# Merged prologues for the projections of a two-block model, with the layer-norm rows on GpSimd behind the last low part

## The reference, cut to what matters

```python
y = gelu(ssm(u) + d_skip * u)
z = y * sigmoid(y @ w_glu + b_glu)
return z @ w_out                      # end of the S5 mixer
z = silu(layernorm(conv(z), ln_g, ln_b))
return z @ w_out + b_out              # end of the convolution mixer
```

## Time and the profile before

| what | us |
|---|---|
| median of the runs | 3826.11 |
| lowest and highest of three | 3824.54, 3830.32 |
| the profiled execution | 3831.06 |
| its span in the trace | 3829.3 |

### The profile page before, as it was taken

One profiled execution on the slowest core, in us unless ns is written; L12 is line 12 of the kernel. 1 busy time (PEld: TensorE's weight loads), 2 busy tenths in 40 slices (PEclk: granted clock), 3 DMA queues, 4 the chain that ended last, 5 costly groups with the idle time before them and its releaser, 6 DMA issues. The chain is left out here.

```text
span 3829.3 us, 64659 instructions
## 1 busy us (share of the span) xinstructions
PE 3380.1 (88%) x20742; PEld 2962.7 (77%) x20742; DVE 2483.6 (65%) x4673; ACT 1672.9 (44%) x3310; POOL 1252.5 (33%) x1096
## 2 busy tenths in 40 slices
PE   8988699999459998798899999987888889999997
PEld 7963489898349986598678999976668877899996
DVE  7979578786958644569954555554355986455555
ACT  4430344445034453344744444444344465444443
POOL 2426112120612100038863333320002976433333
PEclk9985699999579998899999999988688999999999
DMA  5520278685028642344055555544113413555554
GB/s 181 192 89 0 80 258 322 236 326 185 6 100 304 232 163 96 121 140 151 11 170 170 183 186 185 185 150 140 39 55 127 154 44 132 169 185 185 185 186 148
DMA packets 163122, 590.78 MB, mean 154 GB/s; under 512 B 18596, under 2 KB 19364, under 8 KB 162728
## 3 DMA queue, kind: packets, MB, share of 16 engines
q1 hardware_dynamic: 143824, 521.92, 40.1%
q10 hardware_dynamic: 19160, 67.18, 4.7%
HBM read 587.96 MB, written 1.06 MB: 154 GB/s over the span
## 5 line engine op out<-in xcount | busy, mean ns | idle before, releaser
L314 PE MATMUL ps<-hT,parts 128*128 128x256 f32 x12864 | 1630.1, 287 | 108.4 <-DVE parts L138 53.4
L314 PEld LDWEIGHTS ps<-hT,parts 128*128 128x128 f32 x12864 | 1610.7, 195 | 146.5 <-DVE parts L138 58.4
L138 DVE TENSOR_TENSOR parts<-ring,parts 128x512 fp32r<-128x512 f32 x1786 | 1187.4, 700 | 603.3 <-ACT parts L133 594.3
L133 ACT ACTIVATE parts<-ring 128x512 fp32r<-128x512 f32 x1930 | 1156.8, 628 | 624.8 <-PE ps L314 584.8
L314 PE MATMUL ps<-parts,gatedT 128*128 128x512 f32 x4128 | 1008.7, 397 | 8.0 <-DVE parts L138 7.9
L314 PEld LDWEIGHTS ps<-parts,gatedT 128*128 128x128 f32 x4128 | 760.2, 189 | 174.8 <-POOL gatedT L982 8.3
L1118 POOL TENSOR_TENSOR gatedT<-acted,iota 128x256 fp32r<-128x256 f32 x264 | 197.2, 747 | 1434.3 <-PE ps L314 1166.7
L1089 ACT ACTIVATE acted<-ps 128x256 f32<-128x256 f32 x264 | 102.1, 387 | 594.6 <-PE ps L314 594.6
L1121 POOL TENSOR_TENSOR gatedT<-acted,gatedT 128x256 fp32r<-128x256 f32 x264 | 311.1, 1178 | 20.7
L1102 DVE TENSOR_TENSOR acted<-acted,big 128x256 f32<-128x256 f32 x176 | 74.9, 426 | 361.2 <-ACT acted L1089 361.2
L314 PE MATMUL ps<-parts,hT 128*128 128x512 f32 (+2 forms) x1056 | 245.4, 396 | 66.4 <-DVE parts L138 66.4
(11 more groups left out here) (294 smaller groups left out, 2420.0 us busy)
## 6 DMA issues: line engine op xcount, KB each, us to landing
ring<-wts SPq DMA_DIRECT2D x965, 512.0 KB, 3.4
big<-mod_wts ACTq DMA_DIRECT2D x112, 512.0 KB, 5.0
big<-rows SPq DMA_DIRECT2D x15, 512.0 KB, 5.3
big<-mod_bias ACTq DMA_DIRECT2D x14, 512.0 KB, 5.6
big<-mod_rows SPq DMA_DIRECT2D x4, 512.0 KB, 4.6
big<-peer_keys SPq DMA_DIRECT2D x2, 1024.0 KB, 5.1
x<-x_in SPq DMA_DIRECT2D x1, 1024.0 KB, 5.2
big<-s_bc ACTq DMA_DIRECT2D x4, 256.0 KB, 3.2
```

Source lines behind the costliest of these rows:

```text
L133: act.activation(self.part(n, half, 0), self.raw(n, half), ACT.Copy).then_inc(self.hi_done, 1)
L138: v.tensor_tensor(self.part(n, half, 1), self.raw(n, half), self.part(n, half, 0).bitcast(F32), ALU.subtract).then_inc(self.lo_done, 1)
L314: last = pe.matmul(out, a(x), b(y), start=start and x + y == 0, stop=stop and x == 1)
```

## The change

It has these parts:

1. `turn(n)` is false for n under 5, so the additions and all loads but the first two of each feed-forward come later.
2. `ModEntry`: even pieces get their value from ACT, odd pieces from DVE (a new step, `e_odd`), and the turned pieces lie in other banks, so that the two engines read different ones. `e_turned` counts four pieces instead of two.
3. The layer-norm rows on POOL wait for the eighth low part (`e_lo`), not for the transposes.
4. 22 warm matmuls instead of 18, 24 where there is a layer norm.
5. `SplitEntry` can make sum and gelu piece by piece, splits the first weight tile at its start if nothing did, and the second one after the fifth piece. `project_rows` takes an entry.
6. S5: sum, gelu and split become the entry of the sigmoid projection; the gating product is made per piece beside it (`finish`); it splits one tile ahead; the rows projection gets a `SplitEntry`. The rows projections of convolution and NSA get one too.
7. The stage before NSA's query projection splits the first tile of that projection ahead.

```diff
@@ -60,7 +60,7 @@
...
 HELD = 40
-WARM = 18
+WARM, WARM_LN = 22, 24
 GATES = (2, 5, 10, 13)
@@ -398,7 +398,7 @@
...
     def __init__(self, k, pre, post=False, coef=1.0, bias=False):
-        self.k, self.pre, self.post, self.coef, self.bias = k, pre, post, coef, bias
+        self.k, self.pre, self.post, self.coef, self.bias, self.more = k, pre, post, coef, bias, None
@@ -507,13 +507,16 @@
...
-    sems = "e_gained e_squared e_rooted e_updated e_inverse e_normed e_turned e_value e_hi e_lo e_dve e_rows"
+    sems = "e_gained e_squared e_rooted e_updated e_inverse e_normed e_turned e_value e_odd e_hi e_lo e_dve e_rows"
...
     def turned(self, kc):
-        return self.k.ps[:, kc // 2, (kc % 2) * T:(kc % 2) * T + T]
+        at = kc // 2 % 2 * T
+        return self.k.ps[:, kc // 4 + kc % 2 * 2, at:at + T]
@@ -546,14 +549,24 @@
...
                 k.w.split_hi(act, first + n)
-            for kc in range(KC + 1):
-                if kc < KC:
-                    act.wait_ge(s["e_turned"], kc // 2 + 1)
-                    act.activation(self.value(kc), self.turned(kc), ACT.Identity, scale=k.gain[:, self.norm, 0, kc:kc + 1],
-                                   bias=k.gain[:, self.norm, 1, kc:kc + 1]).then_inc(s["e_value"], 1)
-                if kc:
-                    act.wait_ge(s["e_value"], kc)
-                    act.activation(k.hT[:, 0, kc - 1, :], self.value(kc - 1), ACT.Copy).then_inc(s["e_hi"], 1)
+            def even(kc):
+                act.wait_ge(s["e_turned"], kc // 4 + 1)
+                act.activation(self.value(kc), self.turned(kc), ACT.Identity, scale=k.gain[:, self.norm, 0, kc:kc + 1],
+                               bias=k.gain[:, self.norm, 1, kc:kc + 1]).then_inc(s["e_value"], 1)
+            def high(kc):
+                if kc % 2:
+                    act.wait_ge(s["e_odd"], kc // 2 + 1)
+                else:
+                    act.wait_ge(s["e_value"], kc // 2 + 1)
+                act.activation(k.hT[:, 0, kc, :], self.value(kc), ACT.Copy).then_inc(s["e_hi"], 1)
+            even(0)
+            even(2)
+            for kc in range(0, KC, 2):
+                high(kc)
+                high(kc + 1)
+                if kc + 4 < KC:
+                    even(kc + 4)
@@ -598,12 +611,16 @@
...
             for kc in range(KC):
+                if kc % 2 == 0:
+                    v.wait_ge(s["e_turned"], kc // 4 + 1)
+                    v.tensor_scalar(self.value(kc + 1), self.turned(kc + 1), k.gain[:, self.norm, 0, kc + 1:kc + 2],
+                                    k.gain[:, self.norm, 1, kc + 1:kc + 2], ALU.mult, ALU.add).then_inc(s["e_odd"], 1)
                 v.wait_ge(s["e_hi"], kc + 1)
...
         def _(pe):
-            warm(k, pe, first, WARM)
+            warm(k, pe, first, WARM_LN if ln else WARM)
             for tt in range(TT):
@@ -614,13 +631,13 @@
...
                     last = pe.transpose(self.turned(kc)[:, tt * P:(tt + 1) * P], k.x[:, tt, kc * P:(kc + 1) * P], k.ident[:, :])
-                    if tt == TT - 1 and kc % 2 == 1:
+                    if tt == TT - 1 and kc % 4 == 3:
                         last.then_inc(s["e_turned"], 1)
...
             if ln:
-                pool.wait_ge(s["e_turned"], 4)
+                pool.wait_ge(s["e_lo"], KC)
                 for n, op in ((1, ALU.mult), (2, ALU.add)):
@@ -638,24 +655,47 @@
...
-    sems = "e_hi e_lo"
-    def __init__(self, k, src):
-        self.k, self.src, self.more = k, src, None
+    sems = "e_sum e_func e_hi e_lo"
+    def __init__(self, k, src, other=None):
+        self.k, self.src, self.other, self.more = k, src, other, None
...
     def enter(self, s, block, first, done):
-        k, src = self.k, self.src
+        k, src, other = self.k, self.src, self.other
...
         def _(act):
-            for n in range(done, 2):
-                k.w.split_hi(act, first + n)
+            def gelu(kc):
+                act.wait_ge(s["e_sum"], kc + 1)
+                act.activation(src[:, kc, :], src[:, kc, :], ACT.Gelu_apprx_tanh).then_inc(s["e_func"], 1)
+            if done < 1:
+                k.w.split_hi(act, first)
+            if other is not None:
+                gelu(0)
             for kc in range(KC):
+                if other is not None:
+                    if kc + 1 < KC:
+                        gelu(kc + 1)
+                    act.wait_ge(s["e_func"], kc + 1)
                 act.activation(k.hT[:, 0, kc, :], src[:, kc, :], ACT.Copy).then_inc(s["e_hi"], 1)
+                if kc == KC // 2 and done < 2:
+                    k.w.split_hi(act, first + 1)
...
         def _(v):
+            def add(kc):
+                v.tensor_tensor(src[:, kc, :], src[:, kc, :], other[:, kc, :], ALU.add).then_inc(s["e_sum"], 1)
+            if other is not None:
+                add(0)
+                add(1)
+            if done < 1:
+                k.w.split_lo(v, first)
             for kc in range(KC):
+                if other is not None and kc + 2 < KC:
+                    add(kc + 2)
                 v.wait_ge(s["e_hi"], kc + 1)
@@ -668,10 +708,12 @@
...
-def splitting(k, block, first, n, after=None, act_first=None, entry=None, ahead=0):
+def splitting(k, block, first, n, after=None, act_first=None, entry=None, ahead=0, beside=None):
...
     done_hi = max(done, 2) if entry else done
+    if isinstance(entry, SplitEntry):
+        done = max(done, 1)
     k.w.split_to = first + n + ahead
@@ -696,9 +738,18 @@
...
                 k.w.split_lo(v, first + j, i)
-        rounds(v, n, RING, tile)
+        if beside:
+            for f in range(n):
+                if f >= done:
+                    k.w.split_lo(v, first + f)
+                beside(v, f)
+        else:
+            rounds(v, n, RING, tile)
         if ahead:
             k.w.split_lo(v, first + n)
+        if beside:
+            for f in range(n, n + 3):
+                beside(v, f)
@@ -729,7 +780,7 @@
...
-def project_columns(k, n, evacuate, early=(), entry=None):
+def project_columns(k, n, evacuate, early=(), entry=None, ahead=0, finish=None):
@@ -753,17 +804,26 @@
...
             evacuate(act, f, k.ps[:, 4 + f % 4, 0:T]).then_inc(s["stored"], 1)
-            if entry and isinstance(entry, ModEntry) and entry.more and f < KC:
+            if entry and entry.more and f < KC:
                 entry.more_columns(act, s, f)
-        splitting(k, block, first, n, after, entry=entry)
-def project_rows(k, groups=1, evacuate=None, start=True, stop=True, ahead=0, late=()):
+        def finished(v, f):
+            if f >= 3:
+                v.wait_ge(s["stored"], f - 2)
+                finish(v, f - 3)
+        beside = finished if finish else None
+        splitting(k, block, first, n, after, entry=entry, ahead=ahead, beside=beside)
+def project_rows(k, groups=1, evacuate=None, start=True, stop=True, ahead=0, late=(), entry=None):
...
     first = k.w.take(n)
-    with stage(k, "stored") as (s, block):
+    with stage(k, "stored " + (entry.sems if entry else "")) as (s, block):
+        if entry:
+            entry.enter(s, block, first, k.w.split_before(first))
         @block.sync
@@ -775,6 +835,8 @@
...
                     pe.wait_ge(s["stored"], 4 * (g - 1))
+                if entry:
+                    pe.wait_ge(s["e_lo"], f + 1)
                 row_product(k, pe, first + f, lambda tt, half: k.ps[:, 4 * (g % 2) + 2 * tt + half, :],
@@ -786,7 +848,7 @@
...
                         evacuate(act, g, tt, half, k.ps[:, 4 * (g % 2) + 2 * tt + half, :]).then_inc(s["stored"], 1)
-        splitting(k, block, first, n, after if evacuate else None, ahead=ahead)
+        splitting(k, block, first, n, after if evacuate else None, ahead=ahead, entry=entry)
@@ -828,7 +890,7 @@
...
     def turn(self, n):
-        return n % 3 != 1
+        return n >= 5 and n % 3 != 1
@@ -1438,25 +1500,12 @@
...
-    with stage(k, "sum") as (s, block):
-        @block.vector
-        def _(v):
-            v.tensor_tensor(yT, yT, cy, ALU.add).then_inc(s["sum"], 1)
-        @block.scalar
-        def _(act):
-            act.wait_ge(s["sum"], 1)
-            act.activation(yT, yT, ACT.Gelu_apprx_tanh)
-    split_columns(k, yT)
-    project_columns(k, KC, lambda act, f, ps: act.activation(uT[:, f, :], ps, ACT.Sigmoid, bias=col(k, "s5_b_glu", f)))
-    with stage(k, "gated") as (s, block):
-        @block.vector
-        def _(v):
-            v.tensor_tensor(yT, yT, uT, ALU.mult).then_inc(s["gated"], 1)
-    split_columns(k, yT)
-    project_rows(k, ahead=1, late=row_loads(k, "post01"))
+    def gate(v, f):
+        v.tensor_tensor(yT[:, f, :], yT[:, f, :], uT[:, f, :], ALU.mult)
+    project_columns(k, KC, lambda act, f, ps: act.activation(uT[:, f, :], ps, ACT.Sigmoid, bias=col(k, "s5_b_glu", f)),
+                    entry=SplitEntry(k, yT, cy), ahead=1, finish=gate)
+    project_rows(k, ahead=1, late=row_loads(k, "post01"), entry=SplitEntry(k, yT))
@@ -1536,8 +1585,7 @@
...
```

(11 more changed lines are left out.)

## The result

| | median us | lowest, highest | runs | span in the profile |
|---|---|---|---|---|
| before | 3828.22 | 3824.54, 3830.39 | 4 | 3829.3 |
| after | 3784.34 | 3781.10, 3786.17 | 4 | 3779.3 |

The ratio is 0.9885, with a 95% interval of 0.9868 to 0.9903: 43.9 us faster by the medians, where 45.2 was forecast. The interval is 6 to 7 us to either side. The two profiled executions differ by 50.0, since that of before was one of the slower ones of its kernel and that of after the fastest of its own. So I compare steps: the time from one landmark of PE (first warm matmul of a stage, first product) to the next, in both traces. The step of a feed-forward runs from its first warm matmul to that of the next stage, the step of a layer-norm entry from its first warm matmul to the first matmul behind its projection.

A forecast was written before the change was run, and what follows sets the result against it. PE, busy 88% of the span, was taken as the bound, with gains only from its idle or half-clock time. Terms 16.3 + 8.1 + 10.6 + 10.7 - 0.5 = 45.2 us, off the median 3826.11, gave 3781, range 3766 to 3800.

The forecast's parts named there:

- Part 1: Three feed-forward starts: with slots 0 to 4 empty, PE's gap before the second tile goes; 16.3 us gained.
- Part 2: Three layer-norm entries: rows moved behind the last low part hold up weight splits instead; 2.7 us each, 8.1 gained.
- The first rival: Layer-norm entries: the splits don't contend with the rows, three times 3.7 us more, 3770; 12%.
- Part 3: End of S5: 4.3 us from the entry with sum and gelu, 6.3 at the rows projection; 10.6 together.
- Part 4: Prologues of convolution (3.3 us), NSA's output (3.5) and NSA's query projection (3.9): PE starts earlier; 10.7 gained.
- Part 5: Retention's entry: four more warm matmuls and waiting for four pieces delay the transposes; -0.5 us.
- The feed-forward starts did not stay held: Rival: feed-forward starts stay held by first loads in ACT's queue or the ring; their gain is 4, 3793 us; 15%.
- the clock did come back behind the trickles: Rival: in projections behind layer norms the clock stays at half behind the new trickles; slower, some 3835 to 3875 us; 2%.
- the one in which the change mostly does nothing: Rival: each prologue's gain is taken by the next ring wait or the clock; under 7.7 us, 3820 to 3830; 3%.

The follow-up runs named there:

- the repetition: After itself run a second time, nothing changed: 3783.01 us, ratio to before 0.9890.
- the reverse experiment: Before with only the three feed-forward starts given the new turn (slots 0 to 4 left empty): 3812.69 us, ratio to before 0.9963.
- the kernel of half rows: After with each of POOL's four layer-norm rows cut into two halves, one released behind each of stored tiles 2 to 9: 3764.97 us, ratio to before 0.9839.

## Why the prediction came out right

**Part 1** was right in its mechanism and in the size of the gaps. To the 97th product the three starts became 7.2, 4.4 and 6.8 us shorter; 7.2, 4.4 and 6.3 were worked out. Next come the wait of 2.17 us and the 48 products that take 6.0 or 7.5 us behind it. The prediction took 1.6 off for them, and at the first start alone. There it was right: 6.02 in before, 7.51 after. At the third the drop stood in before already, 7.52, and is in after too. The second had 7.49 in before and 6.02 in after, and these 1.5 us are luck: in the repetition the drop is back, and the step is 203.19. From the 145th product to the next stage the three took 169.3, 169.0 and 169.4 us in before and 169.0 each in after, so the additions that moved to the stages' ends cost nothing. That makes 19.1 in the traces for 16.3, and 14 by the medians of the reverse experiment.

**Part 2**: the rows' place and the alternation were as worked out. A half tile came every 2.79 us (2.75), the last low part 16.6 us after the entry's start (16.65), and the new wait alone gave 8.9 us (8.1). Tile 3 started 28.4 us after the first warm matmul in each entry; 1641.7 to 1642 meant 28.4 to 28.7. What was short in the sum is the other end: in before tile 3 started 31.9, 32.5 and 31.7 us after it, where 1644.8 meant 31.5. At the first entry the sum had PE at the full pace from 1638.9, and the clock was still at 0.50 behind that:

```profile
1638.80:1640.70 1.90, 1.90 (x10) 1.90 (x10) 0.95 (x2) 1.42 (x3) 0.00 (x0) 0.50 0.85 276
```

That end makes up 1.8 of the 2.6 us by which the entries gained more than forecast. Of the 10.7, 8.9 come with the wait alone, and the 1.8 more are the entry's other edits, the odd pieces on DVE and the warm matmuls. The first rival, splits that don't contend, is refuted by the eight splits of 13.66 us. A lone row of 2.41 us held DVE up for 1.80, and in the alternation one split got through for each row. With this the trace agrees with the rule of the Trainium skill (SBUF — State Buffer, section "SBUF: two separate sides") that a DVE instruction with two SBUF inputs and a GpSimd one that reads SBUF take a shared port pair in turn, each for its whole length.

**Part 3**: forecast 4.3 and 6.3. Undoing them cost 4.8 and 7.0; the whole step gave 12.7. The sigmoid projection ended 6.1 us earlier in its step, which is where the surplus is, and the wait behind it fell by 6.2. That wait ahead of the rows projection was worked out as 3.65 and was 3.71. The table load lies on the path as I said, but for 1.05 us instead of 1.5: without it ACT waits 1.22 at the stage's boundary in place of 0.75 behind the load, so 0.47 of the load lay in a wait that ACT has there anyway. The Trainium skill (ScalarE: Activation LUTs, section "What ACT_TABLE_LOAD costs") gives about 2.66 us for a switch; by it, as an estimate, that wait would have been about 5. The trace does not agree: the load took 1.28, the next activation started 1.30 after the load did, and the wait was 3.71.

**Part 4**: the waits of convolution and output fell by 3.25 each (3.3 and 3.5). At the query the sum was about right (3.4 against 3.9) and the reason was not: I gave the gain to the tile split ahead. The experiment without that split has the same step, and in it PE's wait is 3.67 where it was 7.19. The gain is from `SplitEntry`'s new order, which splits the second weight tile in the midst of the columns.

**Part 5**: -0.3, for -0.5.

**The total.** The terms add up to 53.3 with the output at 3.25, against 45.2. The medians show 43.9 and, measured once more, 43.1. So the three largest terms were larger in the traces than forecast, and the total was not. 2.9 of the surplus went in the attention stage of the profiled execution. For the rest, one profile of each kernel is compared with medians of other executions. The forecast's closeness is in part luck.

The whole times say less of the parts than the steps do. Each against the before beside it, undoing a part cost 9.6 us (the turn), 0.8 (the rows' wait), -1.6 and -2.2 (the two halves of S5) and 1.9 (convolution, output and query), where the steps say 13.5, 8.2, 4.8, 7.0 and 5.2. Only the turn and the rows' wait were also put into before alone, where they gave 14.2 and 6.2. So for the turn the cause is shown in whole times both ways, for the rows' wait one way, in before; for the other parts it is shown in PE's waits and steps alone.

The feed-forward starts did not stay held, and the clock did come back behind the trickles (the row of 1.00 above), so neither of these two rivals holds, and 43.9 us rules out the one in which the change mostly does nothing. Its mechanism, a gain that the clock takes back later, stays possible for a part of S5's gain.

## What to carry to other kernels

When an engine's bulk work steps on another's, moving it behind the critical pieces is a part of the gain: here 8.2 us of the 23.9 that the rows cost where they stood. Find out how much the chain that it then meets can spare for each tile, and cut the work into pieces that cost less than that: here 0.7 us against 0.8 to 1.2. Work that waits on a load does not belong ahead of its queue's urgent work at a stage's start, however small it is. And before the gain of an edit is booked to one of its lines, that line is to be taken out alone: the query's early split gave nothing that the step shows.

## What was not expected of the hardware

With the same instructions in it, and less the 3.25 us of the output's wait where a kernel has that, the attention stage took 137.0 to 137.4 us in eight profiles, 139.6 to 140.0 in five, and 147.2 in one. The stage in windows, first in before with the new turn (the 147.2), then in the kernel of half rows:

```profile
2687.00:2837.00 150.00, 126.94 (x551) 86.06 (x551) 71.74 (x220) 51.85 (x184) 0.00 (x0) 0.60 0.01 2
```

```profile
2654.00:2791.00 137.00, 117.33 (x552) 80.09 (x552) 70.45 (x219) 50.94 (x185) 0.00 (x0) 0.66 0.01 3
```

PE is busy for 9.6 us more at a mean clock of 0.60 instead of 0.66, so nearly all the difference goes with the clock, and the edit changes no instruction of that stage. Whether it depends on the execution or on when the stage begins is open: the second run of after gave the same 139.7 as the first. One profile of this kernel tells nothing under 3 us of a stage with such gaps in PE's work, unless the wait in question is read by itself.
